# A two-block transformer kernel: MLP sums kept feature-major and added in pairs, and a different opening

## The reference

```python
def rms_norm(x, g):
    xf = x.astype(jnp.float32)
    y = xf * lax.rsqrt(jnp.mean(xf * xf, axis=-1, keepdims=True) + NORM_EPS)
    return (y * g.astype(jnp.float32)).astype(x.dtype)

def sqrelu_mlp(xn, w1, w2):
    return jnp.square(jax.nn.relu(xn @ w1)) @ w2
...
h = h + sqrelu_mlp(rms_norm(h, mlp_norm[layer]), mlp_w1[layer], mlp_w2[layer])
```

## Time and profile before

| | us |
|---|---|
| median of 3 runs | 1596.53 (1594.31 to 1600.73) |
| profiled execution | 1600.82 |
| its span | 1598.9 |
| PE busy | 1437.6 (90%) |
| DVE busy | 1059.0 (66%) |
| ACT busy | 883.2 (55%) |
| POOL busy | 440.5 (28%) |

### The profile page before, as it was taken

The page is one execution under the profiler, slowest core; times in us unless marked ns, Lnnn a source line. Parts: engine busy times, 40 slices in busy tenths (PEclk is TensorE's granted clock), DMA queues, the critical chain, the costliest instruction groups (busy, mean ns, idle before and its releaser), DMA issues. The chain is left out here.

```text
span 1598.9 us, 26385 instructions
## 1 busy us (share of the span) xinstructions
PE 1437.6 (90%) x9598; PEld 1180.1 (74%) x9622; DVE 1059.0 (66%) x1664; ACT 883.2 (55%) x1702; POOL 440.5 (28%) x437
## 2 busy tenths in 40 slices
PE   5996999999988999989888779898898989799998
PEld 5885877768767777769877667777777779587775
DVE  4794766666655766646999745667576666376664
ACT  4433645456556554447988655454565466454453
POOL 3000632343003433324887100003000003073322
PEclk9997999998987999989999989999999989999999
DMA  7230555553822555534343322224434335145551
GB/s 299 106 129 3 185 189 202 187 185 113 204 80 82 193 198 186 184 132 159 132 158 141 123 87 101 103 106 156 140 127 142 129 129 187 41 181 195 187 202 59
DMA packets 35305, 233.55 MB, mean 146 GB/s; under 512 B 3840, under 2 KB 6912, under 8 KB 7936
## 3 DMA queue, kind: packets, MB, share of 16 engines
q1 hardware_dynamic: 30816, 223.75, 38.3%
q10 hardware_dynamic: 3216, 4.19, 1.7%
q0 software_dynamic: 1168, 4.20, 0.9%
HBM read 227.93 MB, written 4.19 MB: 145 GB/s over the span
## 5 line engine op out<-in xcount | busy, mean ns | idle before, releaser
L1515 DVE TENSOR_TENSOR w_lo<-raw,w_hi 128x1024 bf16<-128x1024 f32 x420 | 539.6, 1287 | 233.5 <-ACT w_hi L960 229.4
L960 ACT CAST w_hi<-raw 128x1024 fp32r<-128x1024 f32 x420 | 437.5, 1045 | 266.9 <-PE ps L389 113.3
L383 PE MATMUL ps<-xa_both,w_hi 128*128 128x256 f32 x1040 | 273.7, 302 | 31.0 <-ACT w_hi L960 11.8
L384 PE MATMUL ps<-xa_both,w_hi 128*128 128x256 f32 x1040 | 257.2, 286 | 0.0
L383 PEld LDWEIGHTS ps<-xa_both,w_hi 128*128 128x128 f32 x1040 | 204.9, 197 | 40.5 <-issue 16.3
L384 PEld LDWEIGHTS ps<-xa_both,w_hi 128*128 128x128 f32 x1040 | 205.3, 197 | 0.5
L423 PE MATMUL ps<-xa_both,w_hi 128*128 128x512 f32 x768 | 204.7, 407 | 0.1
L442 PE MATMUL ps<-w_hi,xb_both 128*128 128x512 f32 x384 | 167.1, 435 | 0.0
L2141 POOL TENSOR_SCALAR arena<-arena 128x256 f32<-128x256 f32 x96 | 86.6, 902 | 284.8 <-DVE arena L1583 284.8
L383 PE MATMUL ps<-xb_both,w_hi 128*128 128x256 f32 x576 | 149.8, 299 | 13.6 <-DVE xb_both L1528 7.9
L389 PE MATMUL ps<-xa_bf,w_lo 128*128 128x256 bf16 x1040 | 141.3, 281 | 21.5 <-DVE w_lo L1515 21.5
(11 more groups left out here) (294 smaller groups left out, 2351.3 us busy)
## 6 DMA issues: line engine op xcount, KB each, us to landing
raw<-weights SPq DMA_DIRECT2D x210, 1024.0 KB, 4.8
band<-arena ACTq DMA_DIRECT2D x1, 3072.0 KB, 36.5
arena<-band POOLq DMA_DIRECT2D x8, 256.0 KB, 3.2
arena<-gla_masks SPq DMA_DIRECT2D x1, 1088.0 KB, 15.1
H<-x_t SPq DMA_DIRECT2D x1, 1024.0 KB, 5.1
arena<-mem_t POOLq DMA_DIRECT2D x1, 1024.0 KB, 5.3
arena<-band POOLq DMA_DIRECT2D x8, 128.0 KB, 2.8
out_t<-H ACTq DMA_DIRECT2D x8, 128.0 KB, 2.1
```

The lines of the kernel that those rows point to most:

```text
L383: mm(ps[:, bank, 0:T], w_hi[:, s, k], X.hi[:, k], start=k == 0, stop=False)
L384: mm(ps[:, bank, 0:T], w_hi[:, s, k], X.lo[:, k], start=False, stop=False)
L960: nc.scalar.copy(w_hi[:, j % HI_SLOTS].rearrange("p k n -> p (k n)"), raw[:, j // 2 % RING, j % 2]).then_inc(hi_done, 1)
L1515: TT(w_lo[:, j % HI_SLOTS].rearrange("p k n -> p (k n)"), raw[:, j // 2 % RING, j % 2], w_hi[:, j % HI_SLOTS].rearrange("p k n -> p (k n)" ...
```

## The change

**MLP, up.** `up_chunk` goes; the up chunks are plain ones (16 + 8 matmuls of 256 columns, `hi` and `lo` into the same half bank). DVE reads 256 columns and makes max(x, 0) x rstd in one pass (`m_relu`), POOL only squares. So the norm is applied at once, and in the first group DVE waits for `rstd_done` before its first read. The statistics matmul is the one of 256 columns, not the two of one column each.

**MLP, down.** Weights are stationary again. The down weights are stored in blocks in the order `DOWN`: chunks 0 to 3 of a group cover k = 0, 1 and then 2, 3 for output slices 0 to 3 and 4 to 7; chunks 4 to 7 cover k = 4 to 7 for one pair of output slices each. The sums stand feature by feature in banks 4 to 7, two slices per bank. After down chunk 4 + p of the last group pair p is complete, and DVE adds it straight to H. Copies to SBUF and transposes go, and so do `rtok2`, `m_tok` and two semaphores.

**Opening.** SP loads the 8 columns of `a_norm` first, then H in halves, slab 0, the other parameters, and the rest as before. ACT writes all eight `hi` operands, cuts chunks 0 and 1, writes the eight `bf` operands, cuts chunk 2. PE runs the float32 parts of chunks 0 and 1, then both bf16 parts, chunk 2, the statistics, chunk 3. POOL sums the squares of H in seven passes over 512 columns and one over 256.

**Addresses.** Tensors begin at multiples of 32 bytes. `rtok2` took 32 bytes; `gains` is widened from 8 to 16 columns, 32 bytes more. So `arena`, XA and XB stay where they were (`xa_both` at 186176, a multiple of 64), and of the named buffers only `hn_sqb` (100128 to 100096), `hn_rb` and `gains` move, by 32 bytes.

The order on ACT at the opening, before: from its first operand on. `xa_both` is XA's hi and lo, `xa_bf` its bf16 part.

The diff, cut to its core:

```diff
+DOWN = [[(k, n) for k in (j // 2 * 2, j // 2 * 2 + 1) for n in range(j % 2 * 4, j % 2 * 4 + 4)] for j in range(4)]
+DOWN += [[(k, n) for n in (2 * p, 2 * p + 1) for k in range(4, 8)] for p in range(4)]
...
-        rtok2 = sb("rtok2", [P, NT])
...
-        gains = sb("gains", [P, 8])
+        gains = sb("gains", [P, 16])
...
-            sp.dma_start(H[:], x_d).then_inc(in_done, 16)
-            sp.dma_start(par[:], par_d).then_inc(par_done, 16)
+            sp.dma_start(pcol("a_norm", 0, KC), par_d[:, 0:KC]).then_inc(norm_in, 16)
+            for half in range(2):
+                sp.dma_start(H[:, 4 * half:4 * half + 4], x_d[:, 4 * half:4 * half + 4]).then_inc(in_done[half], 16)
             for s in range(RING):
                 sp.dma_start(raw[:, s].rearrange("p a b -> p (a b)"), w_d[s]).then_inc(slab_in[s], 16)
+                if s == 0:
+                    sp.dma_start(par[:, KC:], par_d[:, KC:]).then_inc(par_done, 16)
...
+            def down_chunk(c, slot, j, build, first, last):
+
+                s, ready = slot % HI_SLOTS, {0: (0, 1), 2: (2, 3), 4: (4, 5, 6, 7)}.get(j, ())
                 pe.wait_ge(hi_done, c + 1)
+                for i, (k, n) in enumerate(DOWN[j]):
+                    if k in ready and n == DOWN[j][0][1]:
+                        pe.wait_ge(XB.lo_done, KC * build + k + 1)
+                    opens = first and k == 0 and n % 2 == 0
+                    mm(down_sums(n), w_hi[:, s, i], XB.hi[:, k], start=opens, stop=False)
+                    mm(down_sums(n), w_hi[:, s, i], XB.lo[:, k], start=False, stop=False)
                 pe.wait_ge(lo_done, c + 1)
...
                 def group(g, first, last):
                     c = c0 + 16 * g
                     for j in range(8):
-                        up_chunk(c + j, o + j, x_build if first and j == 0 else None)
+                        chunk(c + j, o + j, XA, x_build if first and j == 0 else None)
                         if first and j == 0:
-                            stats(nu, False, True)
+                            stats(nu, True, False)
                     if first:
                         pe.wait_ge(rstd_done, nu + 1)
                     for j in range(8):
                         down_chunk(c + 8 + j, o + j, j, xb_build0 + g, first, last)
-                        if last and j == 4:
-                            turn(0)
-                    if last:
-                        turn(1)
...
-            chunk(0, 0, XA, XA_GLA)
+            for c in range(2):
+                chunk_hi(c, c, XA, XA_GLA)
+            for c in range(2):
+                chunk_rest(c, c, XA, XA_GLA)
+            chunk(2, 2, XA, None)
             stats(0, True, True)
-            chunks(1, 3, XA, None)
+            chunk(3, 3, XA, None)
...
                 def final(pair):
-                    act.wait_ge(bank_free, c0 + 60 + pair + 1)
+                    act.wait_ge(bank_free, c0 + 56 + 2 * pair + 2)
                     for n in (2 * pair, 2 * pair + 1):
                         operand(X, build, n, H[:, n], pcol(gain, n))
...
                     for j in range(8):
-                        if last and j == 4:
-                            act.wait_ge(gemm_done, c + 12)
-                            for t in range(NT):
-                                to_sbuf(t, 0)
                         cut_hi(c + 8 + j + AHEAD, o + j + AHEAD)
                         if j == 0:
                             hidden(g, 7)
-                        if last and X is not None and j in (5, 6):
+                        if last and X is not None and j >= 5:
                             final(j - 5)
-                    if last:
-                        act.wait_ge(gemm_done, c + 16)
-                        to_sbuf(0, 1)
-                        if X is not None:
-                            final(2)
-                            final(3)
+                    if last and X is not None:
+                        final(3)
...
-            act.wait_ge(in_done, 16)
+            act.wait_ge(norm_in, 16)
+            for k in range(KC):
+                act.wait_ge(in_done[k // 4], 16)
+                A(XA.hi[:, k], H[:, k], ACT.Copy, scale=pcol("a_norm", k)).then_inc(XA.hi_done, 1)
+            for c in range(2):
+                cut_hi(c, c)
+            for k in range(KC):
+                A(XA.bf[:, k], H[:, k], ACT.Copy, scale=pcol("a_norm", k)).then_inc(XA.bf_done, 1)
+            cut_hi(2, 2)
             act.wait_ge(par_done, 16)
...
                 def final(pair):
-                    dve.wait_ge(turned, 4 * m + pair + 1)
-                    TT(H[:, 2 * pair:2 * pair + 2], ps[:, pair, :].rearrange("p (n t) -> p n t", n=2), H[:, 2 * pair:2 * pair + 2],
-                       ALU.add).then_inc(bank_free, 1)
+                    dve.wait_ge(gemm_done, c0 + 60 + pair + 1)
+                    h = H[:, 2 * pair:2 * pair + 2]
+                    TT(h, down_pair(pair), h, ALU.add).then_inc(bank_free, 2)
...
-                        V.tensor_reduce(m_sum[:, j % 2], ps[:, (o + j) % BANKS, :].rearrange("p (a t) -> p t a", a=2), AX.X,
-                                        ALU.add).then_inc(bank_free, 1 if j < 7 else 5 if last else 9)
+                        if first and j == 0:
+                            dve.wait_ge(rstd_done, nu + 1)
+                        STT(m_relu[:, j % 2], got(c + j, o + j), 0.0, rstd[:], ALU.max, ALU.mult).then_inc(bank_free, 9 if j == 7 and not last else 1)
...
             for k in range(KC):
                 operand_lo(XA, k + 1, k, H[:, k], pcol("a_norm", k))
-                if k < AHEAD:
-                    cut_lo(k, k)
+            for c in range(AHEAD):
+                cut_lo(c, c)
...
+            def first_squares():
+
+                for i in range(4):
+                    pool.wait_ge(in_done[i // 2], 16)
+                    h = H[:, 2 * i:2 * i + 2]
+                    G.tensor_tensor(x_squares[:, min(i, 1)], h, h, ALU.mult).then_inc(sq_step, 1)
```

114 lines of the change are left out of this document (36 added, 78 removed).

## The result

| | median of runs | runs | profiled execution | its span |
|---|---|---|---|---|
| before | 1598.63 us | 4 (1594.31 to 1602.72) | 1600.82 us | 1598.9 us |
| after | 1583.49 us | 4 (1579.73 to 1584.75) | 1579.73 us | 1577.9 us |

The ratio is 0.9902, with a 95% interval of 0.9883 to 0.9922: 15.1 us less. The sum of the prediction was 15.2, its time 1581.3 us.

What follows compares the result with a forecast made beforehand. Inside an MLP only PE's pace was taken to count; PE idles or runs at half pace at the opening and MLP ends. Gains 4.7 + 3.1 + 3.0 + 3.35 + 1.0 = 15.2 us, giving 1581.3 us, range 1573 to 1590.

Steps and rivals of the forecast that it cites:

- Pace: PE's 192 MLP chunks: 2.72 us each instead of 2.736, as in the plain chunk; gain 3.1 us, bounds 0 to 5.
- the turn: Last group of each MLP: PE's transposes of the first half go, 0.99 us each, 3.0 us in three MLPs.
- the 31 ns: MLP matmuls: the skill page's figures would make two short matmuls cost 31 ns more than a wide one, some 60 us.
- the slower rival: MLP chunks: fixed cost for every short matmul with its weight load; at 12 ns each, 1604 us. Chance 0.05.
- The end of the third MLP: Kernel's end: pairs 0 to 2 added and stored during the last three chunks; gain 3.35 us, bounds 2.9 to 3.8.
- The opening: Start to fourth chunk: DVE's lo operands and POOL's passes taking turns decide; fourth chunk at 25.2, gain 4.7 us.
- opening in full: Opening: turns leave DVE the first places, or the clock rises early; gain 19.5 in all, 1577 us. Chance 0.20.
- The ends of the first two MLPs: Statistics somewhat earlier, after pair adds slowed by engines' turns; gain 1.0 us for both, bounds -1.5 and +10.
- T: PE's end at an MLP's end, from which later times count; taken as 355.45 in the first MLP before.
- The turns on ACT and DVE: First two MLP ends: weight cuts, pair adds and operand writes wait in program order, 4.6 us per pair, not 2.72.
- MLP ends in full: First two MLP ends: adds ready per pair during the last chunks; saves up to 9 more, 1572 us. Chance 0.07.
- Gives less: Opening about 2, later statistics at both MLP ends, no gain in pace: 6.8 us, 1590 us. Chance 0.15.

Runs made afterwards that it cites:

- open_alone: The kernel before with the new opening alone, its MLPs as before; ratio to before 0.9968 (0.9951 to 0.9984).
- squares_late: After, with POOL's squares of the input waiting until DVE has written all eight lo operands; ratio to before 0.9909 (0.9880 to 0.9937).
- stats_later: squares_late with PE's statistics matmuls behind the fourth chunk instead of ahead of it; ratio to before 0.9884 (0.9866 to 0.9903).
- wide_up: After, with 8 matmuls of 512 columns instead of 16 of 256 in the up chunks' hi part, lo products left out of the sums; one run, 1583.21 us.
- gains_8: After, with gains 8 elements wide instead of 16, so the operand sets lie 32 bytes lower; median 1600.76 us, ratio to before 1.0007.
- pair_order: After, with ACT cutting weights before writing pair operands and DVE adding pair 3 earlier at the first two MLP ends; ratio to before 0.9872.

## Why the prediction was right, point by point

**Pace.** Forecast 3.1 for pace and 3.0 for the turn, bounds 0 to 5 and 2.7 to 3.1. The three stretches gave 1.92, 1.92 and 1.81, the same in ten profiles with after's MLP code. In the first, the turn is 0.89 by the same starts in before (345.70 to 349.31, less 2.72), so pace 3.0 and turn 2.7. The step was right: the plain chunk's pace holds where the half bank changes, and neither the 31 ns weighed beside it nor the slower rival (12 ns per short matmul) shows anywhere.

**The end of the third MLP.** Forecast 3.35 (2.9 to 3.8). From chunk 419 on, before and open_alone took 8.51 and 7.98, the kernels with the new end 4.66 to 4.76: 3.6. The add began 0.1 us after PE's end where I took 0.4; the span ended 3.6 after it, not 4.5.

**The opening.** Forecast 4.7 (fourth chunk at 24.5 to 25.9). In the eight profiles with this opening unchanged, its bf16 part starts at 26.00 to 27.57, mean 26.8, against 31.72 in the two with the old one: 4.9. The spacing of the lo operands was 1.18, not 1.3; POOL ended at 15.1. PE started at 10.84, not 9.9, which cost nothing since the last lo operand set the pace. The two bf16 parts start at 19.03, the forecast's 19.0, and are at full pace from there, a little before its earliest case (19.5). The rival "opening in full" is refuted as the change stands, and squares_late shows why. But it also shows that my price for it, 9.0, was too high: without turns PE was ready 3.6 us sooner, and other waits then took all of it; stats_later kept 3.0 of it to the z block and lost 1.9 again.

**The ends of the first two MLPs.** Forecast 1.0 for both together. The turns on ACT and DVE were right to 0.2 us: adds after 3.3, 7.9, 12.5 and 14.3 us by my working, 3.2, 7.7, 12.7 and 14.4 in the trace, counted from 336.97. POOL's fifth square came at T + 4.6 (4.4), but its last four squares took 7.5 us, not 7.2, so the statistics came at 12.1, not 11.5. My T of before was early, too: with PE's end taken as in after (start of the last bf16 part, 354.77, and 0.9), before's statistics came at T + 12.2. So the mechanism gained 0.1 us, not 0.9. Yet the stretch 95 to 98 is 1.9 us shorter, since behind the statistics PE was at full clock. Before, then after, four us each:

```profile
367.00:371.00 4.00, 3.44 (x14) 0.50 0.61 207
```

```profile
357.00:361.00 4.00, 3.73 (x31) 1.00 0.72 260
```

That repeats in six profiles with this code (19.05 to 19.07), but not in wide_up (21.22) and gains_8 (21.31), which have the same code there and the statistics at T + 12.1 and 11.9. In wide_up, about as far behind PE's end as the second of these rows:

```profile
361.00:365.00 4.00, 4.00 (x18) 0.50 0.71 264
```

So the 1.9 us are the clock's, they can be absent with the same code at that place, and what decides isn't shown; I had no term for it. At the second end the two kernels with the old code took 28.22 and 26.64. The same six with the new took 27.75 to 27.87, between 0.4 gained and 1.2 lost, with the statistics at T + 11.4 against 10.9 before; gains_8 took 27.26 and wide_up 24.12. Here the clock differs the other way round, after first and then wide_up:

```profile
696.00:700.00 4.00, 4.00 (x27) 0.50 0.66 242
```

```profile
703.00:707.00 4.00, 4.00 (x41) 0.93 0.70 238
```

That my 1.0 came near the 1.5 us of the table is luck: the earlier statistics that it stood for gave 0.1 at one end and cost 0.5 at the other, and the clock gave the rest.

**The rivals.** "MLP ends in full" named its own reason against it, ACT's order, and pair_order shows that reason to be real; but even without it 2.1 us per end come, not the 4 to 5 of my 9, for POOL is behind it. "Gives less" is excluded by the interval: its 6.8 us would be a ratio of 0.996, and the interval ends at 0.9922.

**Sum.** 4.9 + 3.0 + 2.7 + 3.6 + 1.9 - 0.4 (mean of the two) = 15.7 us by the table, 15.1 by the medians. The 1.9 in it is the clock's, at the first MLP end. The other 5 of the 21.0 us between the two profiles are the clock in chunks 16 to 32 (3.1) and small differences of the same kind. The 4.3 us by which the profiled execution of before lay above its median I had only set aside. Of these, 1.9 can be named as the same stretch (96.24, against a mean of 94.4 in the 13 other profiles), and 1.6 as the second end (28.22 against open_alone's 26.64).

**What I gave nothing.** That the operand sets keep their addresses stood in one half sentence, at 0. It was right only because they do: 32 bytes less cost 13.6 us. The rivals had no such case.
